# A three-block kernel with product-key experts: routing on two heads at a time with 136 sums kept, and expert indices worked out on GpSimd

## The reference

```python
sc = jnp.einsum('thcd,chnd->thcn', q, sub_keys)     # 2 halves x 128 keys
top_s, top_i = lax.top_k(sc, 16)
cand_s = top_s[:, :, 0, :, None] + top_s[:, :, 1, None, :]
cand_i = top_i[:, :, 0, :, None] * 128 + top_i[:, :, 1, None, :]
best_s, best_pos = lax.top_k(cand_s.reshape(T, 8, 256), 16)
idx = jnp.take_along_axis(cand_i.reshape(T, 8, 256), best_pos, axis=-1)
g = jax.nn.softmax(best_s, axis=-1)
pre = jnp.einsum('td,thkd->thk', xt, u[idx])
coef = g * jax.nn.gelu(pre, approximate=False)
return jnp.einsum('thk,thkd->td', coef, v[idx])     # u, v: 16384 x 1024
```

## Time and profile before

| | before |
|---|---|
| median of 3 runs | 2208.19 us (2195.73 to 2212.18) |
| profiled execution, span from first to last instruction | 2225.7 us |
| TensorE busy | 1932.8 us, 87% |
| VectorE busy | 1420.4 us, 64% |
| GpSimd busy | 950.8 us, 43% |
| ScalarE busy | 546.8 us, 25% |
| mean granted TensorE clock | 0.912 |

### The profile page before, as it was taken

How to read it: one execution, slowest core, us unless ns; L and a number is a source line. 1 busy time by engine, 2 the same in 40 slices (tenths; PEclk the granted TensorE clock), 3 DMA queues, 4 the chain that set the end, 5 groups by cost and what they waited for, 6 DMA issues and landing times.

```text
span 2225.7 us, 22232 instructions
## 1 busy us (share of the span) xinstructions
PE 1932.8 (87%) x7602; PEld 1232.6 (55%) x7602; DVE 1420.4 (64%) x3218; ACT 546.8 (25%) x1520; POOL 950.8 (43%) x814
## 2 busy tenths in 40 slices
PE   6999999878998997687688767999999999986848
PEld 5677666576865673455556566544467544432313
DVE  1111225446788975689976788999789976544454
ACT  2112034411111110123332157500058400011101
POOL 2000000010333353666745256433868775457765
PEclk9999998788998998885698789999999999998969
DMA  5322244255786586997879777899998999989998
GB/s 174 132 91 104 104 158 150 85 194 194 269 307 218 202 291 237 365 374 252 296 280 342 265 273 230 283 358 363 396 382 310 359 409 409 409 347 353 384 399 302
DMA packets 190624, 614.86 MB, mean 276 GB/s; under 512 B 18096, under 2 KB 18096, under 8 KB 190512
## 3 DMA queue, kind: packets, MB, share of 16 engines
q0 software_dynamic: 111168, 403.64, 49.3%
q1 hardware_dynamic: 76400, 202.92, 24.7%
q10 hardware_dynamic: 2944, 6.89, 0.9%
HBM read 610.22 MB, written 3.15 MB: 276 GB/s over the span
## 4 chain that ended last, share of the span: by engine, by line
PE 66%; DVE 13%; DMA 6%; issue 6%; POOL 4%; ACT 4%; another core or an unknown queue 1%; ACTq 0%; SPq 0%; DVEq 0%
PE ps L1702 65%; DVE sb_arena L1173 5%; POOL sb_arena L652 3%; DMA sb_arena<-in_peer_u,sb_idx 3%; ACT sb_arena L1029 1%; DMA sb_wring<-in_w_out 1%; DMA sb_gains<-in_norm_g 1%; DMA sb_wring<-in_w_in 1%; DVE sb_arena L1312 1%; DVE sb_arena L1638 1%; DMA sb_wring<-in_w_up_attn 0%; POOL sb_wring L652 0%; DMA sb_arena<-in_peer_v,sb_idx 0%; DVE sb_arena L1644 0%
## 5 line engine op out<-in xcount | busy, mean ns | idle before, releaser
L652 POOL DMA_INDIRECT sb_arena<-in_peer_u,sb_idx x470 | 607.1, 1292 | 1046.4 <-DVE sb_idx L1163 496.0
L1702 PE MATMUL ps<-sb_wring,sb_arena 128*128 128x512 f32 (+2 forms) x1632 | 702.0, 591 | 45.2 <-DVE sb_arena L1540 19.9
L1173 DVE CUSTOM_DVE_ANT_0 sb_arena<-sb_arena 128x1024 f32<-128x1024 f32 x470 | 561.8, 1221 | 86.0 <-DMA sb_arena<-in_peer_u,sb_idx 75.9
L1702 PEld LDWEIGHTS ps<-sb_wring,sb_arena 128*128 128x128 f32 x1632 | 313.9, 194 | 422.8 <-issue 367.7
L1702 PE MATMUL ps<-sb_arena,sb_wring 128*128 128x256 f32 (+2 forms) x2688 | 514.4, 353 | 21.6 <-issue 12.3
L1702 PEld LDWEIGHTS ps<-sb_arena,sb_wring 128*128 128x128 f32 x2688 | 449.8, 200 | 75.1 <-issue 18.9
L1702 PE MATMUL ps<-sb_arena 128*128 128x64 f32 (+9 forms) x1968 | 337.6, 322 | 60.1 <-DVE sb_arena L1644 17.5
L1702 PEld LDWEIGHTS ps<-sb_arena 128*128 128x128 f32 (+4 forms) x1968 | 270.0, 194 | 123.9 <-issue 75.0
L652 POOL DMA_INDIRECT sb_arena<-in_peer_v,sb_idx x192 | 208.5, 1086 | 119.7 <-issue 50.0
L1702 PE MATMUL ps<-sb_arena,sb_poolw 128*128 128x512 f32 (+1 forms) x424 | 206.2, 627 | 55.1 <-issue 33.1
L1202 DVE SCALAR_TENSOR_TENSOR sb_arena<-sb_arena,sb_coef 128x1024 f32<-128x1024 f32 x90 | 115.7, 1286 | 124.4 <-DMA sb_arena<-in_peer_v,sb_idx 94.2
(11 more groups left out here) (236 smaller groups left out, 1409.1 us busy)
## 6 DMA issues: line engine op xcount, KB each, us to landing
sb_wring<-in_peer_v SPq DMA_DIRECT2D x128, 512.0 KB
sb_wring<-in_w_in SPq DMA_DIRECT2D x52, 1024.0 KB, 7.5
sb_wring<-in_peer_w_q SPq DMA_DIRECT2D x32, 1024.0 KB, 7.3
sb_wring<-in_w_o SPq DMA_DIRECT2D x16, 1024.0 KB, 7.7
sb_wring<-in_w_out SPq DMA_DIRECT2D x8, 1024.0 KB, 12.5
sb_arena<-in_peer_u,sb_idx POOLq DMA_INDIRECT x470
sb_arena<-in_x ACTq DMA_DIRECT2D x8, 512.0 KB, 7.2
sb_wring<-in_w_up_pool SPq DMA_DIRECT2D x4, 1024.0 KB
```

The costliest lines, as they stand in the source:

```text
L652: nc.gpsimd.indirect_dma_start(gathered[buf(n)], None, table, bass.IndirectOffsetOnAxis(ap=idx[:, t, at_:at_ + 1], axis=0))\
L1173: nc.vector.tensor_tensor_reduce(out=gathered[buf(n)], in0=gathered[buf(n)], in1=xn[:, t % TG, :], scale=1.0, scalar=0.0, op0=ALU.mult, op ...
L1702: return nc.tensor.matmul(o, l, r, start=start, stop=stop)
```

## The change

`prep_pair(m)` takes the place of `prep_top(k)` and routes two heads of one tile in 8 steps. Sums of pairs are made for the first key with all 16 of the second half, and for the other 15 with the first 8: 136 in place of 256. (A pair further out has at least 16 that are no smaller.) The positions are 16-bit, and VectorE stops at shift and mask (L1212, L1213 of the kernel after). The rest is `indices(m)` on GpSimd: 36 instructions for each pair of heads, of which 33 wait for the one before (`link`), and the first waits for `places_done`. Four sets of positions can be on their way (`ROUTES`); from the fifth pair on `prep_pair` waits until `idx_ready` shows that a set is free. `INDICES_AT` says ahead of which u chunk of GpSimd's queue a pair is turned into indices. `split` now waits for `idx_ready`. The scratch of the routing is laid out anew. The rest, the numbers in `side(n)` among it, is as before.

```diff
+EDGE = TOPK // 2
+SUMS = TOPK + (TOPK - 1) * EDGE
+ROUTES = 4
...
-                eng.wait_ge(idx_ready, CHUNKS)
+                eng.wait_ge(top_done, CHUNKS)
             elif b in OVER:
                 eng.wait_ge(d_used, NK)
+        INDICES_AT = {0: (0, 1, 2, 3), 2: (4,), 3: (5,), 4: (6,), 5: (7,), 16: (8,), 18: (9,), 20: (10,), 21: (11, 12),
+                      23: (13, 14), 29: (15,)}
...
+            def indices(m):
+                t, c = divmod(2 * m, H)
+                gp.wait_ge(places_done, m + 1)
+                nc.gpsimd.tensor_copy(topif.rearrange("p a b -> p (a b)"), topi[:, m % ROUTES, :])
+                link(nc.gpsimd.tensor_copy(posf2.rearrange("p a b -> p (a b)"), posab[:, m % ROUTES, :]))
+                block_, column_ = [posf2[:, n, :].rearrange("p (h r) -> p h r", h=2) for n in range(2)]
+                nc.gpsimd.tensor_scalar(digits[:, :, 0, :], block_, 1.0, 0.0, ALU.subtract, ALU.max)
+                link(nc.gpsimd.tensor_scalar(wide[:], posf2[:, 0, :], 1.0, float(EDGE), ALU.is_equal, ALU.mult))
+                link(nc.gpsimd.tensor_tensor(digits[:, :, 1, :], wide.rearrange("p (h r) -> p h r", h=2), column_,
+                                             ALU.add))
+                for h in range(2):
+                    for q in range(2):
+                        link(nc.gpsimd.tensor_tensor(onehot[:], digits[:, h, q].unsqueeze(2).to_broadcast([P, TOPK, TOPK]),
+                                                     iota[:, 0:TOPK].unsqueeze(1).to_broadcast([P, TOPK, TOPK]),
+                                                     ALU.subtract))
+                        link(nc.gpsimd.tensor_scalar(onehot[:], onehot[:], 0.0, None, ALU.is_equal))
+                        link(nc.gpsimd.tensor_tensor(onehot[:], onehot[:], topif[:, 2 * h + q, :].unsqueeze(1)
+                                                     .to_broadcast([P, TOPK, TOPK]), ALU.mult))
+                        for n in (8, 4, 2):
+                            link(nc.gpsimd.tensor_tensor(onehot[:, :, 0:n], onehot[:, :, 0:n], onehot[:, :, n:2 * n],
+                                                         ALU.add))
+                        link(nc.gpsimd.tensor_tensor(digits[:, h, q].unsqueeze(2), onehot[:, :, 0:1], onehot[:, :, 1:2],
+                                                     ALU.add))
+                link(nc.gpsimd.tensor_scalar(digits[:, :, 0, :], digits[:, :, 0, :], float(NK), None, ALU.mult))
+                link(nc.gpsimd.tensor_tensor(digits[:, :, 0, :], digits[:, :, 0, :], digits[:, :, 1, :], ALU.add))
+                nc.gpsimd.tensor_copy(idx[:, t, c * TOPK:(c + 2) * TOPK].rearrange("p (h r) -> p h r", h=2),
+                                      digits[:, :, 0, :]).then_inc(idx_ready, 2)
...
             for n in range(GATHERS):
                 kind, k, j = order_of_dmas[n]
                 if kind == "d":
                     continue
+                if kind == "u" and j == 0:
+                    for m in INDICES_AT.get(k, ()):
+                        indices(m)
                 if kind == "u" and j == 0:
                     gp.wait_ge(idx_ready, k + 1)
                 wait_buffer(gp, n)
...
-            def prep_top(k):
...
+            def prep_pair(m):
+                t, j = divmod(m, H // 2)
+                dve.wait_ge(prep_evac, NP * t + PREP.index(("s", j)) + 1)
+                if m >= ROUTES:
+                    dve.wait_ge(idx_ready, 2 * (m - ROUTES) + 2)
+                scores = [scores_of(t)[:, 4 * j + q, :] for q in range(4)]
+                ti = topi[:, m % ROUTES, :].rearrange("p (a b) -> p a b", a=4)
+                pn = posn.rearrange("p (a b) -> p a b", a=2)
+                for q in range(4):
+                    last = nc.vector.max(tops[:, q, 0:8], scores[q])
                 link(last)
+                yield
+                for q in range(4):
+                    nc.vector.max_index(ti[:, q, 0:8], tops[:, q, 0:8], scores[q])
                 yield
                 for half in range(2):
+                    for q in range(2):
+                        last = nc.vector.match_replace(spare2[:, q, :], tops[:, 2 * half + q, 0:8],
+                                                       scores[2 * half + q], BELOW)
+                    if half:
+                        last.then_inc(top_done, 2)
+                        dve.wait_ge(top_done, 2 * m + 2)
+                    else:
+                        link(last)
+                    for q in range(2):
+                        last = nc.vector.max(tops[:, 2 * half + q, 8:16], spare2[:, q, :])
+                    link(last)
+                    yield
+                    for q in range(2):
+                        last = nc.vector.max_index(ti[:, 2 * half + q, 8:16], tops[:, 2 * half + q, 8:16],
+                                                   spare2[:, q, :])
+                    link(last)
+                pairs_ = tops.rearrange("p (h c) b -> p h c b", c=2)
+                nc.vector.tensor_tensor(cand[:, :, 0:TOPK], pairs_[:, :, 0, 0:1].to_broadcast([P, 2, TOPK]),
+                                        pairs_[:, :, 1, :], ALU.add)
+                link(nc.vector.tensor_tensor(cand[:, :, TOPK:SUMS].rearrange("p h (a b) -> p h a b", b=EDGE),
+                                             pairs_[:, :, 0, 1:TOPK].unsqueeze(3).to_broadcast([P, 2, TOPK - 1, EDGE]),
+                                             pairs_[:, :, 1, 0:EDGE].unsqueeze(2)
+                                             .to_broadcast([P, 2, TOPK - 1, EDGE]), ALU.add))
+                yield
+                for h in range(2):
+                    last = nc.vector.max(best[:, h, 0:8], cand[:, h, :])
+                link(last)
+                for h in range(2):
+                    nc.vector.max_index(pn[:, h, 0:8], best[:, h, 0:8], cand[:, h, :])
+                yield
+                for h in range(2):
+                    last = nc.vector.match_replace(cand2[:, h, :], best[:, h, 0:8], cand[:, h, :], BELOW)
+                link(last)
+                for h in range(2):
+                    last = nc.vector.max(best[:, h, 8:16], cand2[:, h, :])
                 link(last)
                 yield
+                for h in range(2):
+                    last = nc.vector.max_index(pn[:, h, 8:16], best[:, h, 8:16], cand2[:, h, :])
                 link(last)
+                cols = soft[:, t, 2 * j * TOPK:(2 * j + 2) * TOPK].rearrange("p (h r) -> p h r", h=2)
+                nc.vector.tensor_tensor(cols, best[:], best[:, :, 0:1].to_broadcast([P, 2, TOPK]),
+                                        ALU.subtract).then_inc(soft_in, 2)
+                ab = posab[:, m % ROUTES, :].rearrange("p (a b) -> p a b", a=2)
+                nc.vector.tensor_scalar(ab[:, 0, :], posn[:], 3, None, ALU.logical_shift_right)
+                nc.vector.tensor_scalar(ab[:, 1, :], posn[:], EDGE - 1, None, ALU.bitwise_and).then_inc(places_done, 1)
+                topped[0] += 2
...
                 def tops_of(*ks):
-                    for k in ks:
-                        while k % H >= routed[k // H]:
+                    for k in ks[::2]:
+                        while k % H + 1 >= routed[k // H]:
                             yield
-                        yield from prep_top(k)
+                        yield from prep_pair(k // 2)
...
-                pieces = tops_of(*range(20, 29))
+                pieces = tops_of(*range(20, 30))
...
-                pieces = tops_of(*range(29, CHUNKS))
+                pieces = tops_of(*range(30, CHUNKS))
...
             def split():
                 dve.wait_ge(u_used, LATE)
+                dve.wait_ge(idx_ready, EARLY_CHUNKS)
```

78 lines of the change are left out of this document (17 added, 61 removed).

## The result

The change made the kernel slower: 2324.4 us median of 4 runs (2321.41 to 2332.09) against 2206.84 us (2195.73 to 2212.18), a ratio of 1.0544 with a 95% interval of 1.0515 to 1.0572. The forecast was 2287 in a range of 2190 to 2420.

What follows compares the result with a forecast made beforehand. TensorE was taken to bound most of the kernel (busy 87%, 66% of the chain), VectorE some windows. Terms A to G summed to +79 us on the profiled 2225.7, giving 2305 there and 2287 us as median; range 2190 to 2420.

Steps and rivals of the forecast that it cites:

- VectorE's saving: Routing by pairs: some 8 us of 17.7 saved per pair, 130 us over the kernel, mostly where TensorE bounds.
- T: Time of one `indices(m)` block on GpSimd: 18 us, from 3.6 fixed, 7.9 waits and 6.5 elements.
- Beside dots: Time of a GpSimd block standing beside VectorE's dots: 21 us.
- R2: Rival, much slower: GpSimd's operations and VectorE's dots hold each other up, 2385 to 2485 us; chance 0.17.
- A: Ahead of the first gather: four blocks delay it, fourteen rows precede the evacuation in first_dense(1); +32 us.
- B: first_dense(1) and attention(1): rows replace routing steps, blocks 4 to 7 drain the buffers; +40 us.
- C: Last part of second_attention: the early rows are used up, so waits for rows go; -20 us.
- D: Start of the builds: ScalarE's 7.67 us wait for a VectorE dot goes as VectorE's work shortens; -8 us.
- E: First builds: block 9 ahead of chunk 18 is covered by buffers, the block behind begins late; +8 us.
- F: Stage with tiles: GpSimd's rows and about six blocks in series, 249 us in a stage of 225; +24 us.
- G: The rest: block 15 in place of two heads' routing, beside transfers; +3 us.
- R1: Rival, faster: T of 10 us or less, VectorE's saving counts where VectorE bounds; some 2185 us; chance 0.18.

Runs made afterwards that it cites:

- one_input_rows: The change with each row's dot on VectorE replaced by a sum over the gathered row alone; 2275.95 us, ratio 1.0323 to the kernel before.
- four_op_indices: The change with the lookup left out, each GpSimd block only four operations joining top lists rank by rank; 2234.62 us, ratio 0.9988 to the kernel before.
- vector_indices: The change with the lookup back on VectorE, pairs and 136 sums kept, 10 steps a pair; 2254.59 us, ratio 1.0071 to the kernel before.
- change_14_steps: The change with each of the first 8 pairs' routing cut into 14 steps instead of 8; 2304.17 us, ratio 1.0418 to the kernel before.
- four_op_14_steps: The change with four-operation blocks (lookup left out) and 14 steps for each of the first 8 pairs; 2189.28 us, ratio 0.9903 to the kernel before.
- vector_14_steps: The change with the lookup back on VectorE and each pair in 14 steps; 2197.83 us, ratio 0.9966 to the kernel before.
- double_blocks: The change with the four lookups of each GpSimd block worked twice, same result; 2543.56 us, ratio 1.1517 to the kernel before.
- the second trace of before: The kernel before run once more, unchanged, for a trace from another chip; 2215.3 us in its one run.

## Why the prediction came out as it did

The direction, the place and the mechanism were right: blocks in GpSimd's queue ahead of gathers that someone waits for. Taken one by one, against the marks:

- **VectorE's saving, 130 us.** 118 and 120 us are gone from its busy time in the two runs with four-operation blocks, and 104 in the change.
- **T, 18 us.** Measured 18.5 to 19.4 when quiet. The sum was right with wrong parts, which is luck. A linked operation starts 0.07 to 0.10 us after the one before, not 0.24, so the waits are some 3 us and not 7.9. The elements cost more: 0.62, 0.85 and 0.73 us for 256, where 0.10 and 1.5 ns each make 0.48. The two errors cancel. The 0.56 us that the prediction estimated for a two-operand operation of 256 elements is near the 0.62 and 0.73 measured.
- **Beside dots, 21 us.** Low. Those in attention(1) took 22.0 to 23.9, in the stage with tiles 26.2 to 28.4, in the first builds 31.4. Of the blocks that were to stand beside rows, only 12 and 14, each directly behind another, took 18.5, since VectorE had run out of rows by then. R2's mechanism is real: one_input_rows takes the blocks back to 18.5 to 19.7 us. Its 2.2%, about 49 us, hold shorter gathers as well, so they are not a share of the change's loss. The argument against R2, that gathers beside back-to-back dots still take 0.94 us, was wrong: the earlier trace rows has one of 1.68 us at the first dots, and the 470 of the largest group average 1292 ns before the change. I had it as a rival at 0.17 and priced at ten blocks of 30 to 40; it was part of the likeliest case. By the Trainium skill's page ("SBUF — State Buffer", "Who interferes with whom") two-operand VectorE instructions contend with GpSimd's reads and one-operand ones do not. That is what the run shows for the blocks, though it took away the dot's wide write as well, and no run parts the two. Of the gathers' instructions the rows alone tell: they are longer beside dots as well.
- **A, +32: 26.7.** The first row was used 5.0 us after its gather's start, not 8.4, and the fourteen rows came 1.58 us apart (from 572.92 to the last at 593.46), not 1.8. One sentence of this step is doubtful: that with six rows landed already all would cost nothing. No run has just that. In four_op_indices the first gather is at 540.89 (it stands behind pair 3's block), the first row at 548.89, the fourteen rows come 1.97 us apart, and the evacuation is 8 us late; in vector_indices six rows had landed, six stood ahead, and it is 5.5 us late.
- **B, +40: 47.4.** Of the waits for rows the largest was where it was expected, 20.92 us at chunk 5, forecast 21; behind blocks 4, 5 and 6 they were 7.4, none and 9.1 us, forecast 3, 8 and 8. The part for rows in place of routing was set at 9: change_14_steps, which takes it away, has a B 11.7 us shorter, and four_op_indices, which has little else, is at 10.6. To the end of the program the 8-step stream costs 15 to 28 us (15 by the spans of the two traces, 28 by the ratios). Not in the sum at all was that TensorE's matmuls take up to 16 us more there at the lower clock. GpSimd is asked for 108 gathers between the evacuation and the last step of attention(1), where it made 75.
- **C, -20: -7.1. D, -8: -11.1.** C's rows did run out, but the last pair's routing stands in one of its steps, which took 35 us between scans. D's mechanism was wrong: ScalarE still waits 7.06 us for the dot, so the gain lies ahead of it. Nor does it come from the shorter routing. change_14_steps, four_op_14_steps and vector_14_steps have that too, and C and D together are at 8.7, -2.0 and -0.1 us there, while the runs with 8-step pairs have them at -17 to -19 (double_blocks at -8). Both gains go with the rows pulled forward in A and B; that both terms had the right sign and about the right size is luck.
- **E, +8: 14.8.** Block 9 took 31.4 us, not 21. With four-operation blocks E is 0.5, so it is the block's.
- **F, +24: 40.8.** The mechanism was right, GpSimd's work in series. The term counted 80 rows at 1.24 to 1.3 us (102), and there are 99 at 1.18 + 0.30 (147), of which 79 in one group; it counted about six blocks (125), and there are five (118); and it set the 249 us against a stage of 225, where the marks give 229. With four-operation blocks F is 0.0: all of it is the blocks'.
- **G, +3:** -1.5 against the second trace of before.

Together, against the second trace, 107.7 where 79 was forecast (95.5 against the first, and 118 by the medians). The largest misses are F's 17 us, C's 13, and B and E with 7 each. In F it is the count and the pace of the gathers, in E the block's length beside two-operand work. So the direction and place were earned by the argument; the size came out within the range while four of its terms were off by 7 to 17 us.

**R1 was wrong altogether.** It had 2185 for T of 10 or less, from 40 us where VectorE bounds. With blocks of 2 us the ratio is 0.9988. VectorE's saving is worth 0.8 to 1% (four_op_14_steps), and the shorter stream takes most of it back (four_op_indices, on another chip, stands at 0.9988, and at the third picks within 0.1 us of before). That rival forgot that a generator pulled by count changes its order when its steps change.

## What to carry to other kernels

A queue that issues gathers in order is not idle capacity because its busy share is 43%: add up, by stage, what it must issue and what you give it, and compare with the stage's length. Ask what runs beside the moved work. Two-operand instructions on VectorE made a GpSimd block of 18.5 us one of 22 to 31, and a gather's instruction of 0.94 us one of 1.52, before the change as well: the pace of such a queue depends on what VectorE does. Where work is pulled by a count of steps, keep the steps' number when you make them shorter, or set the counts anew: here that was worth 0.9 to 1.3%.

## What the runs showed of the hardware that was not expected

- GpSimd and VectorE hold each other up even where GpSimd's instruction is tiny: a 128x16 addition took 214 ns alone and 644 on average beside picks and dots, and a dot 1460 ns in place of 1221.
- The GpSimd instruction that issues a gather took 0.94 us with no two-operand instruction of VectorE beside it and 1.52 us when it started inside a dot (47 and 266 gathers of the kernel before); with one-operand rows 0.95.
- A linked GpSimd operation starts 0.07 to 0.10 us after its predecessor; a gather behind a computation starts after 0.28 to 0.59 us, behind another gather after 0.30.
- Cutting a block into pieces made it dearer: beside rows all the time, the computing in the stage with tiles took 123 us in place of 104.
